# MLP down projection: all 16 pairs of row blocks by seven products, and a last product that is finished tile by tile

## Chip, core and metric

One core of one Trainium2 chip runs the whole layer in one launch. The metric is the device time of that launch in microseconds (us), lower is better. The time before is the median of three runs; the profile is one further execution with the hardware profiler.

The engines are named as in the profile: PE (TensorE, with PEld for its weight loads), DVE (VectorE), ACT (ScalarE), POOL (GpSimd) and SP (SyncE, which here only issues DMA transfers). SBUF is the on-chip memory of 128 partitions, PSUM the eight banks of 128x512 float32 into which PE sums.

## What is computed

The layer is a streaming encoder step over 1024 prompt rows and 128 sample rows, 1152 tokens of width 1024. The change touches only its last part, which in the reference is one line of `finish`:

```python
u = jnp.square(jax.nn.relu(jnp.einsum('bld,df->blf', rmsnorm(h, g_pre_mlp), w_up)))
return h + rmsnorm(jnp.einsum('blf,fd->bld', u, w_down), g_post_mlp)
```

`w_up` is 1024 x 4096 and `w_down` 4096 x 1024, so `u` is 1152 x 4096. Float32 accuracy is reached with float32r operands: each operand is split into a high part (an ACT copy to float32r) and a low part (the difference, one DVE or POOL subtraction), and each product is three matmuls, high by high, high by low, low by high.

## The kernel before

The 4096 inner columns are 32 blocks of 128. **Up.** The first four blocks (`NCL = 4`) are made classically: `mlp_up_pe` computes them in three chunks of 384 tokens each, `up_square_act` squares them into the two buffers `ust`, and `up_store` writes each to the scratch `c_scr`. The other 28 blocks are 14 pairs (`NPAIR = 14`), each made from seven block products in the manner of Strassen and Winograd: `pair_pe` runs products 1, 6, 7, 5, then the last 128 tokens (`last_tokens_pe`), 4, a turn of those tokens (`last_turn_pe`), 2 and 3. `pair_dve` makes the sums of weights for the next pair, the low parts (`w_low_dve`), and the sums of results (`c22_dve` and others); `last_square_dve` squares the last tokens before the turn. After each pair `out_sums_dve` makes four sums of the squared blocks, and SP stores the pair's buffer to `u_scr`.

While the classical blocks 2 and 3 run on PE, DVE makes the weight and token sums of the first pair (`x_difference_dve`, `x_second_dve`, `x_fourth_dve`, `w_s1_dve` and so on), one instruction after another in the order of the `vector` block.

**Down.** The 14 pairs are contracted with `w_down` by seven products in the order `ZORD = (1, 7, 6, 5, 4, 2, 3)`. Product p runs over all 14 pairs (`z_step_pe`, 98 steps, `ZN = 7 * NPAIR`) into four PSUM banks for tokens 0 to 511, three matmuls each; four of the seven also have one tile for the last 128 tokens. A step is thus 12 or 15 matmuls of 128x512. Four sets of operands (`zop[n % 4]`) go round: SP loads (`z_load_sp`), ACT makes the high parts (`z_hi_act`), DVE the low ones (`z_low_dve`), and `z_out_dve` adds each finished product into the output tiles `yt` during the next product.

**Tail.** The four classical blocks are then contracted classically: `tail_pe` runs 9 token tiles by 2 halves by 4 blocks by 3 matmuls, 216 in all, half a tile at a time. So every half tile has 12 matmuls of its own, and while PE does the next ones, the tile before is finished: `tail_dve` adds the half into `yt`, ACT squares the tile with a row sum, DVE makes the variance and its reciprocal (`norm_var`, L2681 to L2683), ACT the root, DVE one Newton step (`norm_newton`, L2687 to L2689), POOL multiplies by `g_post_mlp` (`end_gain_pool`; DVE does it for the last two tiles), and DVE multiplies by the root and adds the residual `hend` (`end_dve`). SP then stores the tile.

What sets the order: every engine runs its own queue strictly in the order in which the code is written, and waits there on semaphores. There is no scheduler.

Of the kernel before, what the change touches and what calls it, by code (L numbers as in the profile page):

```python
# [5 lines left out]
P = 128  # L6
# [6 lines left out]
D = 1024  # L13
# [27 lines left out]
NTAIL = NCL // 2  # L41
# [158 lines left out]
def layer(nc, I, O, scratch):  # L200
    o_scr, sig_scr, h_scr = scratch
    keep = ExitStack()
    with keep:
# [173 lines left out]
        wr[0] = wr_first + [raw[x][:, 512 * h:512 * h + 512] for x in range(2) for h in range(2)] + wr_late  # L377

        class Operands:
            def __init__(self, k):  # L380
# [7 lines left out]
        sb("before_yt", [P, 1152], ctx=D1)  # L388
# [4 lines left out]
        uraw = [osT_rl[:, 0:TOK], sb("uraw1", [P, TOK], ctx=D1)]  # L393
# [4 lines left out]
        tu = [[sb(f"tu{b}{x}", [P, 2 * TOK], F32R, E1) for x in range(2)] for b in range(2)]  # L398
        td1h = sb("td1h", [P, 2 * D], F32R, E1)
        sb("before_td1l", [P, 3840], ctx=E1)  # L400
        td1l = sb("td1l", [P, 2 * D], F32R, E1)
        sb("before_hend8", [P, 2048], ctx=E1)
        hend8 = sb("hend8", [P, D], ctx=E1)
        jend = sb("jend", [P, D], ctx=E1)
        sb("before_hend", [P, 6400], ctx=E1)
        hend = [sb(f"hend{t}", [P, D], ctx=E1) for t in range(8)] + [hend8]
        gend = sb("gend", [P, D], ctx=E1)
        E1.close()
        yg = raw
        td = [[[wh[0][:, :], wh[1][:, :]], [wl[0][:, :], wl[1][:, :]]],  # L410
              [[T[:, D * x:D * x + D] for x in range(2)] for T in (td1h, td1l)]]
        cum_scr = nc.dram_tensor("cum_scr", (STREAMS * HEADS, PK), F32, kind="Internal").ap()
        c_scr = nc.dram_tensor("c_scr", (NCL * P, TOK), F32, kind="Internal").ap()
        u_scr = nc.dram_tensor("u_scr", (NPAIR * P, UCOL), F32, kind="Internal").ap()
# [61 lines left out]
        u_lo, u_hi, u_down, d_hi, d_lo = sem("u_lo"), sem("u_hi"), sem("u_down"), sem("d_hi"), sem("d_lo")  # L476
        u_out, u_in, d_in, rw_in = ([sem(f"{n}{x}") for x in range(2)] for n in ("u_out", "u_in", "d_in", "rw_in"))
# [5 lines left out]
        yg_done, yg_last = sem("yg_done"), sem("yg_last")  # L483
# [2339 lines left out]
        def up_store(sp, j):  # L2823
            sp.wait_ge(u_lo, U_B + (j + 5 if j < 2 else 3 * j + 3))
            sp.dma_start(c_scr[P * j:P * j + P, :], ust[j % 2]).then_inc(u_out[j % 2], 16)
# [281 lines left out]
        def ust_free(eng, Q, x):  # L3107
            eng.wait_ge(u_out[x], Q.of((32, 16)[x], U0))
# [150 lines left out]
        def pair_sp(sp, Q):  # L3259
            if Q.it is None:  # L3260
                rows = slice(P * Q.n0, P * Q.n0 + P)
            else:
                rows = bass.ds(Q.of(P), P)
# [26 lines left out]
        ZN = 7 * NPAIR  # L3290
# [12 lines left out]
        def zprod(n):  # L3303
            return ZORD[n // NPAIR]
# [19 lines left out]
        def z_load_sp(sp, n):  # L3324
            i, s, k = zprod(n), n % NPAIR, n % 4
# [3 lines left out]
            if n < 4:  # L3329
                sp.wait_ge(q_done, 9 * (NPAIR - 1) + (2, 3, 3, 4)[n])  # L3330
                sp.wait_ge(u_out[0], U0 + 32 * (s + 1))
# [4 lines left out]
            if n == NPAIR - 1:  # L3336
                sp.wait_ge(u_out[0], U1)
                sp.wait_ge(u_out[1], U2)
            rows = slice(P * s, P * s + P)
            for x, b, h in ZLOAD.get(i, ()):  # L3340
                f = P * (NCL + 2 * s + b)
# [5 lines left out]
        def z_sum_dve(v, n):  # L3347
            i, s = zprod(n), n % NPAIR
            to, a, b, op = ZSUM[i]
            v.wait_ge(z_in[n % 4], z_in_at(n))  # L3350
            v.wait_ge(q_low, Z_LOW + z_parts_at(n - NPAIR))
            nc.vector.tensor_tensor(wr[to][s][:, :], wr[a][s][:, :], wr[b][s][:, :], op).then_inc(q_sum, 1)

        def z_hi_act(act, n):
            i, s, Z = zprod(n), n % NPAIR, zop[n % 4]
            act.wait_ge(z_in[n % 4], z_in_at(n))
            if n < 4:
                act.wait_ge(q_done, 9 * (NPAIR - 1) + (2, 3, 3, 4)[n])
            else:
# [4 lines left out]
            nc.scalar.activation(Z.u[0][:, :], Z.uraw[:, :], ACT.Copy).then_inc(q_hi2, 1)  # L3364
            if i in ZLAST:
                nc.scalar.activation(Z.last[0][:, :], Z.lraw[:, :], ACT.Copy).then_inc(q_hi2, 1)

        def z_low_dve(v, n):
            i, s, Z = zprod(n), n % NPAIR, zop[n % 4]
# [4 lines left out]
            nc.vector.tensor_tensor(Z.u[1][:, :], Z.uraw[:, :], Z.u[0][:, :].bitcast(F32), ALU.subtract).then_inc(q_low, 1)  # L3374
            if i in ZLAST:
                v.wait_ge(q_hi2, Z_HI + at_ + 3)
                nc.vector.tensor_tensor(Z.last[1][:, :], Z.lraw[:, :], Z.last[0][:, :].bitcast(F32), ALU.subtract).then_inc(q_low, 1)

        def z_step_pe(pe, n):
            p, s, Z = n // NPAIR, n % NPAIR, zop[n % 4]  # L3380
            i, own, other = zprod(n), ZBANK[p % 2], ZBANK[1 - p % 2]
            start, stop = s == 0, s == NPAIR - 1
# [32 lines left out]

        L_, R_ = slice(0, 512), slice(512, 1024)
# [14 lines left out]
        def z_out_dve(v, p, xs_):  # L3431
# [3 lines left out]
            if xs_[0] == 0:  # L3435
# [626 lines left out]
```

## Time and profile before

| | us |
|---|---|
| time, median of 3 runs (1632.14 to 1632.45) | 1632.45 |
| the profiled execution's own time | 1632.51 |
| its span, first to last instruction | 1630.6 |
| mean granted PE clock over the span | 0.998 |

The engines' busy shares of the span are PE 99%, DVE 65%, ACT 48%, POOL 20%. A start time in a row is counted from the start of the span. A duration of a PE, DVE or ACT instruction can reach into the next one's; from one start to the next is what an instruction costs in a row of them.

### The profile page before, as it was taken

How to read it: one execution, taken by the hardware profiler on the slowest of the kernel's cores; microseconds unless marked ns; L12 is line 12 of the kernel's file. 1: busy time of each engine (PE TensorE's matmuls, PEld its weight loads, DVE VectorE, ACT ScalarE, POOL GpSimd, SP SyncE). 2: the span in 40 equal slices, each digit the busy share in tenths (PEclk: the TensorE clock that was granted, in tenths of full speed). 3: DMA queues.
4: the chain of work that ended last, by engine and by line, in shares of the span. 5: the costliest groups of instructions: out<-in, count | busy, mean ns of one | idle time of the engine just before them, and what ended most of it. 6: DMA issues, size and time to landing. Idle time of an engine off the chain costs nothing.

```text
span 1630.6 us, 27195 instructions
## 1 busy us (share of the span) xinstructions
PE 1614.9 (99%) x9314; PEld 1465.3 (90%) x9314; DVE 1064.4 (65%) x2323; ACT 782.7 (48%) x1643; POOL 329.5 (20%) x539
## 2 busy tenths in 40 slices
PE   8999999999999999999999999999999999999998
PEld 8999999999999999999988998888888888888886
DVE  7567777645888422264455798887787577775657
ACT  6487887865888523341343452222222334344522
POOL 0412312225544322234522100000000000000124
PEclk9999999999999999999999999999999999999999
DMA  5221312322222556654433424433444773353642
GB/s 185 82 63 38 84 48 65 90 91 55 69 73 74 195 193 203 208 194 153 140 122 95 141 82 149 148 122 119 144 134 155 242 241 102 109 171 105 187 157 117
DMA packets 167437, 209.73 MB, mean 129 GB/s; under 512 B 16697, under 2 KB 114361, under 8 KB 167329
## 3 DMA queue, kind: packets, MB, share of 16 engines
q1 hardware_dynamic: 167328, 208.34, 40.1%
q8 instruction: 61, 1.00, 0.3%
q14 instruction: 48, 0.39, 0.1%
HBM read 148.26 MB, written 58.24 MB: 127 GB/s over the span
## 4 chain that ended last, share of the span: by engine, by line
PE 95%; DVE 2%; ACT 2%; issue 0%; DMA 0%; SPq 0%; DVEq 0%; ACTq 0%
PE gb L565 9%; PE gb L3395 6%; PE sc L3395 6%; PE gb L2488 6%; PE gb L1024 5%; PE gb L1026 5%; PE gb L1025 5%; PE gb L3044 5%; PE sc L3044 5%; PE tp L3395 5%; PE tp L3044 5%; PE tp L864 4%; PE sc L2647 3%; PE gb L2870 3%; PE tp L2647 3%; PE gb L3054 2%
## 5 line engine op out<-in xcount | busy, mean ns | idle before, releaser
L534 POOL TENSOR_TENSOR wl<-raw,wh 128x256 fp32r<-128x256 f32 x168 | 123.3, 759 | 299.9 <-ACT wh L516 175.7
L1024 PE MATMUL gb<-Xh,wh 128*128 128x384 f32 (+1 forms) x504 | 173.0, 343 | 0.0
L1025 PE MATMUL gb<-Xh,wl 128*128 128x384 f32 (+1 forms) x504 | 170.8, 339 | 0.0
L1026 PE MATMUL gb<-Xl,wh 128*128 128x384 f32 (+1 forms) x504 | 170.8, 339 | 0.0
L3516 POOL TENSOR_TENSOR wl<-raw,wh 128x1024 fp32r<-128x1024 f32 x2 | 5.3, 2626 | 624.8 <-ACT wh L3507 624.8
L565 PE MATMUL gb<-Xh,wh 128*128 128x384 f32 (+1 forms) x288 | 102.8, 357 | 0.0
L565 PE MATMUL gb<-Xh,wl 128*128 128x384 f32 (+1 forms) x288 | 97.6, 339 | 0.0
L3395 PE MATMUL gb<-zw,zu 128*128 128x512 f32 x378 | 97.2, 389 | 0.0
L565 PE MATMUL gb<-Xl,wh 128*128 128x384 f32 (+1 forms) x288 | 97.2, 338 | 0.0
L1024 PEld LDWEIGHTS gb<-Xh,wh 128*128 128x128 f32 x504 | 94.8, 188 | 0.4
L1025 PEld LDWEIGHTS gb<-Xh,wl 128*128 128x128 f32 x504 | 94.8, 188 | 0.1
L1026 PEld LDWEIGHTS gb<-Xl,wh 128*128 128x128 f32 x504 | 94.8, 188 | 0.0
L3395 PE MATMUL sc<-zw,zu 128*128 128x512 f32 x336 | 89.5, 389 | 0.0
L3395 PE MATMUL tp<-zw,zu 128*128 128x512 f32 x336 | 85.3, 389 | 0.0
L3395 PEld LDWEIGHTS gb<-zw,zu 128*128 128x128 f32 x378 | 70.9, 188 | 14.7
L3363 ACT ACTIVATE zw<-wr 128x512 fp32r<-128x512 f32 x56 | 35.4, 632 | 91.5 <-issue 45.8
L3395 PEld LDWEIGHTS sc<-zw,zu 128*128 128x128 f32 x336 | 63.1, 188 | 13.1
L3395 PEld LDWEIGHTS tp<-zw,zu 128*128 128x128 f32 x336 | 63.1, 188 | 13.1
L3374 DVE TENSOR_TENSOR zu<-zr,zu 128x512 fp32r<-128x512 f32 x98 | 67.1, 684 | 0.0
L3372 DVE TENSOR_TENSOR zw<-wr,zw 128x512 fp32r<-128x512 f32 x56 | 46.0, 822 | 27.0 <-ACT zw L3363 26.7
L2488 PE MATMUL gb<-Oh,wh 128*128 128x384 f32 x188 | 63.2, 336 | 0.2 <-DVE Ol L2437 0.2
L2488 PE MATMUL gb<-Ol,wh 128*128 128x384 f32 x188 | 62.8, 334 | 0.0
(551 smaller groups left out, 4637.6 us busy)
## 6 DMA issues: line engine op xcount, KB each, us to landing
zr<-u_scr SPq DMA_DIRECT2D x98, 256.0 KB, 3.0
raw<-in_w_in SPq DMA_DIRECT2D x70, 256.0 KB, 3.3
u_scr<-ustore SPq DMA_DIRECT2D x28, 576.0 KB, 3.9
u_scr<-ustore SPq DMA_DIRECT2D x14, 768.0 KB, 3.3
sig_scr<-sig SPq DMA_DIRECT2D x16, 576.0 KB, 3.2
raw<-in_w_up SPq DMA_DIRECT2D x36, 256.0 KB, 4.6
kc<-in_cache_fox_k SPq DMA_DIRECT2D x8, 1024.0 KB, 5.5
vc<-in_cache_fox_v SPq DMA_DIRECT2D x8, 1024.0 KB, 7.7
```

The lines of the kernel that those rows point to most:

```text
L534: last = nc.gpsimd.tensor_tensor(wl[U.slot][:, q], raw[U.slot][:, q], wh[U.slot][:, q].bitcast(F32), ALU.subtract)
L565: last = nc.tensor.matmul(bank[:, 0:b - a], w_[U.slot][:, ws], x_[:, k, a:b], start=(k == 0 and j == 0), stop=(k == KT - 1 and j == 2))
L864: last = nc.tensor.transpose(four(rbank[R.slot])[0:n, j, 0:m], src, ident[0:m, 0:m])
L1024: nc.tensor.matmul(bank[:, 0:x1 - x0], wh[U.slot][:, ws], Xh3[:, k, x0:x1], start=(k == 0), stop=False)
L1025: nc.tensor.matmul(bank[:, 0:x1 - x0], wl[U.slot][:, ws], Xh3[:, k, x0:x1], start=False, stop=False)
L1026: last = nc.tensor.matmul(bank[:, 0:x1 - x0], wh[U.slot][:, ws], Xl3[:, k, x0:x1], start=False, stop=(k == KT - 1))
L2488: last = nc.tensor.matmul(bank[:, 0:384], w_[M.U.slot][:, ws], x_[:, 4 * y + k, a:b], start=(k == 0 and j == 0), stop=(k == 3 and j == 2))
L2647: last = nc.tensor.matmul(bank[:, :], m_[:, k, ts], w_[:, hs], start=(k == 0 and j == 0), stop=(k == KT - 1 and j == 2))
L2870: last = nc.tensor.matmul(gb[x][:, 0:384], w_[j % 2][:, ws], x_[:, k, a:a + 384], start=(k == 0 and i == 0), stop=(k == KT - 1 and i == 2))
L3044: last = nc.tensor.matmul(bank[:, :], w_of(i, wp)[:, P * k:P * k + P], x_of(i, xp)[:, k, :], start=(k == 0 and j == 0), stop=(k == 3 and j ...
L3374: nc.vector.tensor_tensor(Z.u[1][:, :], Z.uraw[:, :], Z.u[0][:, :].bitcast(F32), ALU.subtract).then_inc(q_low, 1)
L3395: last = nc.tensor.matmul(bank[:, :], A[a], Z.w[w][:, :], start=(start and j == 0), stop=(stop and j == 2))
```

## The change

All 32 blocks go through the seven products (`ZP = NPAIR + NCL // 2 = 16` pairs, `ZN = 112` steps), and the classical tail is gone with its loads and splits.

1. The first four blocks are still made classically, but as two more pairs: POOL makes the four sums that `out_sums_dve` makes for the others (`up_sums_pool`), and SP stores them into `u_scr`. The squares of blocks 2 and 3 wait for sums and store of blocks 0 and 1, since they share `ust`. ACT squares the first two chunks of block 2 a little later than before, behind a split for the pair.
2. Loads of `w_down` for pairs 14 and 15 have buffers of their own; the last two steps have operands of their own (`EndOperands`).
3. The last step of the last product (`z_group_pe`, `GROUP = 1`) raises a semaphore for each tile, in the order 8, 1, 2, 3, 0.
4. Tiles 4 to 7 (`EARLY`) are complete before the last product; their squares, variances, gains and residuals are put between the steps of the last product. `g_post_mlp` and `hend` are loaded during the last two products. The left halves of the five late tiles are squared and multiplied there too.
5. The five late tiles are finished in `end_late_dve`, one after the other, behind the last product. POOL makes all gains, DVE none.

```diff
+ZP = NPAIR + NCL // 2
+GROUP = 1
...
+        def up_sums_pool(pool, b):
+
+            add = nc.gpsimd.tensor_tensor
+            t1_, t2_ = slice(0, HALF), slice(HALF, SEQ)
+            pool.wait_ge(u_lo, U_B + 6 * b + 6)
+            if b:
+                pool.wait_ge(u_out[0], 16)
+            add(usum[0], ust[0][:, t2_], ust[1][:, t2_], ALU.add).then_inc(uc_sum, 1)
+            pool.wait_ge(uc_sum, 4 * b + 1)
+            add(ust[0][:, t2_], ust[0][:, t1_], ust[0][:, t2_], ALU.subtract).then_inc(uc_sum, 1)
+            pool.wait_ge(uc_sum, 4 * b + 2)
+            add(usum[1], usum[0], ust[0][:, t1_], ALU.subtract).then_inc(uc_sum, 1)
+            pool.wait_ge(uc_sum, 4 * b + 3)
+            add(usum[2], ust[1][:, t1_], usum[1], ALU.subtract).then_inc(uc_sum, 1)
...
-            if j >= 2:
-                act.wait_ge(u_out[j % 2], 16 * (j // 2))
+            if j == 2:
+                act.wait_ge(uc_sum, 3)
+                act.wait_ge(uc_out, 16)
+            elif j == 3:
+                act.wait_ge(u_out[1], 16)
...
-        ZN = 7 * NPAIR
+        ZN = 7 * ZP
...
+        def z_group_pe(pe):
+
+
+            for t in (8,) + ZTILES:
+                for n in range(ZN - GROUP, ZN):
+                    Z = zset(n)
+                    if t == 8:
+                        pe.wait_ge(q_low, Z_LOW + z_parts_at(n))
+                        bank, A = ZBANK[1][1], [l_[:, :] for l_ in Z.last]
+                    else:
+                        bank, A = ZBANK[0][t], [u_[:, P * t:P * t + P] for u_ in Z.u]
+                    for j, (a, w) in enumerate(((0, 0), (0, 1), (1, 0))):
+                        last = nc.tensor.matmul(bank[:, :], A[a], Z.w[w][:, :], start=False, stop=(n == ZN - 1 and j == 2))
+                last.then_inc(z_tile, 1)
...
-        def tail_pe(pe):
-            for b in range(NTAIL):
-                pe.wait_ge(u_down, 2 * b + 2)
-                pe.wait_ge(d_lo, 2 * b + 2)
-                for q in range(6):
-                    if b == 0 and q == 3:
-                        pe.wait_ge(q_step, Z_OUT + z_out_at(7))
-                    last = tail_product_pe(b, ENDB[q], q // 2, q % 2)
-                    if b == NTAIL - 1:
-                        last.then_inc(dn_full, 1)
-            for q in range(6, 2 * TT):
-                pe.wait_ge(dn_free, END_B + q - 5)
-                for b in range(NTAIL):
-                    last = tail_product_pe(b, ENDB[q % 6], q // 2, q % 2)
-                last.then_inc(dn_full, 1)
...
+        END_FROM = 6 * ZP + 4
+        EARLY, LATE = (4, 5, 6, 7), (8,) + ZTILES
+        FINAL = EARLY + LATE
...
+            end_square_act(act, LATE[0], 1)
+            for x in range(1, 5):
+                end_square_act(act, LATE[x], 1)
+                end_root_act(act, LATE[x - 1])
+            end_root_act(act, LATE[4])
...
+            for t in EARLY:
+                pool.wait_ge(sq_b, sq_at(t, 1))
+                nc.gpsimd.tensor_tensor(yt[t][:, :], yt[t][:, :], gend[:, :], ALU.mult).then_inc(yg_done, 1)
+            for h in range(2):
+                for t in LATE:
+                    pool.wait_ge(sq_b, sq_at(t, h))
+                    nc.gpsimd.tensor_tensor(half(yt[t], h), half(yt[t], h), half(gend, h), ALU.mult).then_inc(yg_done, 1)
...
+        def end_late_dve(v):
+
+
+            z_out_last_dve(v, 6)
+            for x in range(5):
+                end_var_dve(v, LATE[x])
+                if x < 4:
+                    z_out_dve(v, 6, (x,))
+                end_newton_dve(v, LATE[x])
+                end_dve(v, LATE[x])
...
@@ -3903,8 +3904,7 @@
             pairs(v, lambda Q: pair_dve(v, Q), NPAIR)
             z_steps_dve(v)
-            z_out_dve(v, 6, range(4))
-            end_group_dve(v, lambda t, h: tail_dve(v, t, h))
+            end_late_dve(v)
...
@@ -3953,9 +3953,8 @@
-            for b in range(NTAIL):
-                for x in range(2):
-                    tail_low_pool(pool, b, x)
+            for b in range(2):
+                up_sums_pool(pool, b)
             end_gain_pool(pool)
```

How the instructions stand, at the places where the order matters. On POOL, from the last residual sum of the stage before (L2754, in the change L2749) to the end of the queue; `tb` and `xr` are the residual's buffers. Before:

```order
L2754 TENSOR_TENSOR tb0<-tb0,xr0 128x1024
L3516 TENSOR_TENSOR wl0<-raw0,wh0 128x1024
L3516 TENSOR_TENSOR wl1<-raw1,wh1 128x1024
L3516 TENSOR_TENSOR td1l<-raw0,td1h 128x1024
L3516 TENSOR_TENSOR td1l<-raw1,td1h 128x1024
L3599 TENSOR_TENSOR raw0<-yt0,gend 128x1024
```

And in the change:

```order
L2749 TENSOR_TENSOR tb0<-tb0,xr0 128x1024
L2825 TENSOR_TENSOR ustore<-ustore 128x512
L2827 TENSOR_TENSOR ustore<-ustore 128x512
L2829 TENSOR_TENSOR ustore<-ustore 128x512
L2831 TENSOR_TENSOR ustore<-ustore 128x512
L2825 TENSOR_TENSOR ustore<-ustore 128x512
L2827 TENSOR_TENSOR ustore<-ustore 128x512
L2829 TENSOR_TENSOR ustore<-ustore 128x512
L2831 TENSOR_TENSOR ustore<-ustore 128x512
L3622 TENSOR_TENSOR yt4<-yt4,gend 128x1024
```

The four splits of the tail's weights are gone; eight half-width sums of the first blocks stand in front of the gains.

On DVE, the end of the queue: `yt` is an output tile, `hend` its residual, `small` the columns of the norm. Before, tiles 7 and 8:

```order
L3606 TENSOR_TENSOR raw1<-yt7,gend 128x1024
L2681 TENSOR_SCALAR small<-small 128x1
L2682 TENSOR_SCALAR small<-small 128x1
L2683 RECIPROCAL small<-small 128x1
L3551 TENSOR_TENSOR yt8<-tp0,yt8 128x512
L2687 TENSOR_SCALAR small<-small 128x1
L2688 TENSOR_SCALAR small<-small 128x1
L2689 TENSOR_SCALAR small<-small 128x1
L3627 SCALAR_TENSOR_TENSOR yt7<-raw1,small,hend7 128x1024
L3551 TENSOR_TENSOR yt8<-tp1,yt8 128x512
L3606 TENSOR_TENSOR raw0<-yt8,gend 128x1024
```

In the change, the turn of tile 1, the second of five late ones:

```order
L3644 SCALAR_TENSOR_TENSOR yt8<-yt8,small,hend8 128x1024
L2676 TENSOR_SCALAR small<-small 128x1
L2677 TENSOR_SCALAR small<-small 128x1
L2678 RECIPROCAL small<-small 128x1
L3517 TENSOR_TENSOR yt2<-tp0,yt2 128x512
L2682 TENSOR_SCALAR small<-small 128x1
L2683 TENSOR_SCALAR small<-small 128x1
L2684 TENSOR_SCALAR small<-small 128x1
L3644 SCALAR_TENSOR_TENSOR yt1<-yt1,small,hend1 128x1024
```

Each late tile's turn holds the addition of the next tile's last product between its reciprocal and its Newton step, and ends in the residual of the whole tile.

On ACT, the end of the queue in the change (L3588 squares half a tile, L3592 is the root):

```order
L3588 ACTIVATE gb0,small<-yt8 128x512
L3588 ACTIVATE gb0,small<-yt1 128x512
L3592 ACTIVATE small<-small 128x1
L3588 ACTIVATE gb0,small<-yt2 128x512
L3592 ACTIVATE small<-small 128x1
L3588 ACTIVATE gb0,small<-yt3 128x512
L3592 ACTIVATE small<-small 128x1
L3588 ACTIVATE gb0,small<-yt0 128x512
```

Tile 8's root stands behind tile 1's square, tile 1's behind tile 2's, and so on. Before, each root followed its own tile's square.

## Rows read from the trace of the kernel before

**Rows 1.** The page, busy time of the engines (share of the span, instructions).

```profile
PE 1614.9 (99%) x9314; PEld 1465.3 (90%) x9314; DVE 1064.4 (65%) x2323; ACT 782.7 (48%) x1643; POOL 329.5 (20%) x539
```

**Rows 2.** Chain that ended last, in order of time, its end: start, length, what.

```profile
1573.67 2.72 PE gb L3522 x12
...
1614.47 2.73 PE sc L3522 x12
...
1617.30 0.06 DVE yt L3551
```

**Rows 3.** Timeline, DVE, to the end: start, length, instruction, [idle before <-releaser].

```profile
1543.84 2.55 DVE L3372 TENSOR_TENSOR zw<-wr,zw 128x512 fp32r<-128x512 f32 x1 [0.27 <-ACT zw L3363]
...
1562.05 0.29 DVE L3377 TENSOR_TENSOR zl<-zs,zl 128x128 fp32r<-128x128 f32 x1
...
1620.24 0.21 DVE L2681 TENSOR_SCALAR small<-small 128x1 f32<-128x1 f32 x1
...
1620.75 0.67 DVE L3551 TENSOR_TENSOR yt<-tp,yt 128x512 f32<-128x512 f32 x1
...
1622.07 1.28 DVE L3627 SCALAR_TENSOR_TENSOR yt<-raw,small,hend 128x1024 f32<-128x1024 f32 x1
1623.27 0.69 DVE L3551 TENSOR_TENSOR yt<-tp,yt 128x512 f32<-128x512 f32 x1
...
1625.14 0.21 DVE L2681 TENSOR_SCALAR small<-small 128x1 f32<-128x1 f32 x1
...
1626.00 0.27 DVE L2687 TENSOR_SCALAR small<-small 128x1 f32<-128x1 f32 x1 [0.27 <-ACT small L3589]
...
1626.75 1.42 DVE L3631 SCALAR_TENSOR_TENSOR yt<-raw,small,hend 128x512 f32<-128x512 f32 x2
```

**Rows 4.** Timeline, ACT, the last tile's second half.

```profile
1623.99 0.63 ACT L3586 ACTIVATE jend<-yt 128x512 f32<-128x512 f32 x1 [1.76 <-DVE yt L3551]
1624.53 0.19 ACT L3586 ACTIVATION_READ_ACCUMULATOR jend<-yt 128x1 f32 x1
1625.77 0.20 ACT L3589 ACTIVATE small<-small 128x1 f32<-128x1 f32 x1 [1.05 <-DVE small L2683]
```

**Rows 5.** Timeline, POOL, last stage: two passes over 128x1024.

```profile
1543.21 2.62 POOL L3516 TENSOR_TENSOR wl<-raw,wh 128x1024 fp32r<-128x1024 f32 x1 [4.17 <-ACT wh L3507]
...
1585.45 2.40 POOL L3599 TENSOR_TENSOR raw<-yt,gend 128x1024 f32<-128x1024 f32 x1 [26.02 <-DVE yt L3551]
```

**Rows 6.** Timeline, all engines, mixing stage: DVE and POOL together.

```profile
740.25 1.84 DVE L2505 SCALAR_TENSOR_TENSOR Ml<-sga,Mh 128x384 f32 x2
...
740.41 1.26 POOL L2514 TENSOR_TENSOR sga<-sga,sgb 128x384 f32<-128x384 f32 x1 [1.06 <-DVE sgb L2498]
```

**Rows 7.** Stretches: PE, PEld, DVE, ACT, POOL busy (instructions), PEclk granted, DMA share.

```profile
935.00:958.00 23.00, 23.00 (x135) 23.00 (x134) 22.69 (x24) 12.17 (x20) 0.00 (x0) 1.00 0.30 98
1624.00:1626.00 2.00, 0.00 (x0) 0.00 (x0) 1.66 (x4) 0.92 (x3) 0.00 (x0) 0.73 0.64 262
```

**Rows 8.** Timeline, ACT, squares that end first-block pairs 0 and 1.

```profile
934.71 0.51 ACT L2886 ACTIVATE ustore<-osT_rl 128x384 f32<-128x384 f32 x1
...
958.85 0.53 ACT L2886 ACTIVATE ustore<-osT_rl 128x384 f32<-128x384 f32 x1
```

**Rows 9.** Timeline, DVE, from the last first-block work into the first pair.

```profile
955.38 1.29 DVE L3036 TENSOR_TENSOR wq<-rw,wq 128x512 fp32r<-128x512 f32 x2
...
964.28 0.69 DVE L3000 TENSOR_TENSOR ss<-raw 128x512 f32<-128x512 f32 x1
...
969.34 0.68 DVE L3183 TENSOR_TENSOR ustore<-tp,vsum 128x512 f32<-128x512 f32 x1
...
972.54 0.43 DVE L3161 TENSOR_TENSOR rs<-rs 128x256 f32<-128x256 f32 x1 [0.59 <-ACT rs L3123]
```

**Rows 10.** Timeline, PE, start of the first pair, and its turn of tokens.

```profile
958.13 0.63 PE L3044 MATMUL sc<-Mh,wq 128*128 128x512 f32 x2
...
974.68 0.38 PE L3060 MATMUL gb<-ident,rs 128*128 128x128 f32 x2
```

More of the change, by code:

```diff
@@ L387, in layer @@
         zop = [Operands(3)]
-        sb("before_yt", [P, 1152], ctx=D1)
+        wr[2] += [sb(f"wr_last{s}", [P, 512], ctx=D1) for s in range(2)]
+        sb("before_yt", [P, 128], ctx=D1)
         yt = [sb(f"yt{t}", [P, D], ctx=D1) for t in range(6)] + yt_last
@@ L392, in layer @@
         sb("before_uraw", [P, 384], ctx=D1)
-        uraw = [osT_rl[:, 0:TOK], sb("uraw1", [P, TOK], ctx=D1)]
+        wr[1] += [sb(f"wr_end{s}", [P, 512], ctx=D1) for s in range(2)]
         D1.close()
@@ L3107, in ust_free @@
         def ust_free(eng, Q, x):
+            if Q.first():
+                eng.wait_ge(uc_out, 32)
             eng.wait_ge(u_out[x], Q.of((32, 16)[x], U0))
@@ L3303, in zprod, with __init__, zset @@
         def zprod(n):
-            return ZORD[n // NPAIR]
+            return ZORD[n // ZP]
+        class EndOperands:
+            def __init__(self, k):
+                side = (wh, wl)[k]
+                self.w = [side[0][:, 0:512], side[0][:, 512:1024]]
+                self.u = [side[1][:, 0:512], side[1][:, 512:1024]]
+                self.last = zlast[k]
+        zend = [EndOperands(k) for k in range(2)]
+        def zset(n):
+            return zend[n - ZN + 2] if n >= ZN - 2 else zop[n % 4]
         def parts_in(n):
@@ L3514, in tail_low_pool @@
-        def tail_low_pool(pool, b, x):
-            pool.wait_ge(d_hi, 2 * b + x + 1)
-            nc.gpsimd.tensor_tensor(td[b][1][x], raw[x][:, :], td[b][0][x].bitcast(F32), ALU.subtract).then_inc(d_lo, 1)
-        def tail_product_pe(b, bank, t, h):
-            for x in range(2):
-                us = slice(TOK * x + P * t, TOK * x + P * t + P)
-                for i, (up, dp) in enumerate(((0, 0), (0, 1), (1, 0))):
-                    last = nc.tensor.matmul(bank[:, :], tu[b][up][:, us], td[b][dp][x][:, 512 * h:512 * h + 512],
-                                            start=(b == 0 and x == 0 and i == 0), stop=(b == NTAIL - 1 and x == 1 and i == 2))
-            return last
@@ new lines, in end_square_act @@
+        def end_square_act(act, t, h):
+            if sq_at(t, h) > TT + 1:
+                act.wait_ge(sq_b, sq_at(t, h) - 1)
+            if t in EARLY:
+                act.wait_ge(q_step, Z_OUT + z_out_at(6))
+            elif h == 0:
+                act.wait_ge(q_step, Z_OUT + z_out_at(6))
+            else:
+                act.wait_ge(q_step, Z_OUT + z_out_at(6) + LATE.index(t) + 1)
+            c = (32, 75)[h] + t
+            nc.scalar.activation(junk_bank[:, :], half(yt[t], h), ACT.Square, accum_out=stat[:, c:c + 1]).then_inc(sq_b, 1)
@@ L3815, in _ @@
             pairs(act, lambda Q: pair_act(act, Q), NPAIR)
[L3816 to L3821 removed]
+            z_steps_act(act)
         @block.vector
@@ L3993, in _ @@
             pairs(pe, lambda Q: pair_pe(pe, Q), NPAIR)
-            for n in range(ZN):
+            for n in range(ZN - GROUP):
                 z_step_pe(pe, n)
-            tail_pe(pe)
+            z_group_pe(pe)
 def tables():
```

263 lines of the change are left out of this document (103 added, 160 removed).

## Prediction

> **What bounds the kernel now.** I read the page first, then the chain, then the two places where the change puts new work. PE is busy for 99% of the span [rows 1], and the end of the chain is nothing but its matmuls [rows 2]: the tail starts at 1573.67, and sixteen half tiles of 12 matmuls each end at 1617.20 (1614.47 + 2.73). That is 43.53 us for 192 matmuls, 0.2267 us each. The last two half tiles end PE's work at 1617.20 + 24 x 0.2267 = 1622.64. The span is 1630.6, so 7.96 us follow the last matmul. Two things can therefore change the time: the number of matmuls (if nobody makes PE wait), and the length of what follows the last one. A third is a new wait of PE at a place where its supplier has no room. The reader is to see in [rows 7] that DVE is such a supplier: from 935 to 958 it is busy for 22.69 of 23.00 us.
>
> **Matmuls removed.** The tail's 216 go. Two more pairs through seven products cost 2 x 7 x 4 x 3 = 168, and 2 x 4 x 3 = 24 for the last tokens, 192 together. 24 fewer, at 0.2267: **-5.44 us**. The tail's splits on ACT, DVE and POOL lay beside PE and give nothing back. Loads grow from 14 to 16 per product at the same rate per step, so I cost them at nothing; the loads run four steps ahead, and if that cover were gone a step would wait for its transfer.
>
> **POOL's sums beside a full DVE.** POOL and DVE cannot both read two SBUF operands. In [rows 6] DVE starts at 740.25 two instructions of 384 columns; POOL starts 0.16 later and ends at 741.67; the DVE pair ends at 742.09, 0.42 behind POOL, after 1.84 us. One of them would need about 0.45 to 0.5 by the 0.60 that 512 columns take from one start to the next [rows 9]. So I read that POOL waited for the first, and the second for POOL. In [rows 3] and [rows 5] POOL works from 1543.21 to 1545.83, and the DVE subtraction of 1543.84 takes 2.55 us, ending 0.56 after POOL, where its like takes 0.69.
>
> The Trainium skill ("SBUF — State Buffer", who interferes with whom) says the same: the port pair is an exclusive lock for a whole instruction, and a DVE instruction with two SBUF inputs contends with a GpSimd instruction that reads SBUF. The trace agrees (2.55 against 0.69 us). The rule speaks against putting sums on POOL where DVE is full.
>
> A POOL pass over 128x1024 takes 2.40 [rows 5]; one over 512 at least half, 1.20, and 1.30 with some fixed cost (384 columns take 1.26 in [rows 6], a wait of about 0.25 among it). I take 1.30. It delays a full DVE by about 0.1 less, 1.19. The first four sums can start when the last square of block 1 ends, 934.71 + 0.51 = 935.22 [rows 8]. Each needs the one before, so they alternate with DVE instructions of 0.6 to 1.2 us and are through by about 944. DVE is then 4 x 1.19 = 4.75 behind. The low part of weight 1, which started at 955.38 [rows 9], would start at 960.1. But the second four sums start when the last square of block 3 ends, 959.4 [rows 8] and some 0.2 later here, so one of them gets in front of it: done at about 962.05. PE began product 1 at 958.13 [rows 10]. It waits about 4.0 us.
>
> The other three sums fall on DVE before it reaches the first pair's weights for the next. From 964.28 on [rows 9] it is 4.75 + 4 x 1.19, less about 1 us that it idled between, so 8.5 us late. `c22_dve` moves from 969.34 to 977.85, and three instructions and one low part later the square of the last tokens starts at 980.4 instead of 972.54 (there it had waited 0.59 for ACT) and ends at 980.8. PE's turn of tokens, 974.68 before [rows 10], stands behind it: PE arrives at 978.7 and goes on at 980.9. PE is thus **+6.2 us** late in all, the first wait being part of it. After that DVE has idle time in each pair and catches up. What is queued behind PE's waits is all of PE's later work. Bounds: 0, if the POOL sums find gaps or their delay is covered; 10, if each sum costs DVE a full alternation. The stores of the sums come at 944 and 968 and are asked for only at `c22_dve`: hidden. SP stands in these stores with the next pair's weight load behind it, which is wanted over 15 us later.
>
> A wait of 4 us can also cost clock. After PE's last matmul (1622.64) the granted clock of the stretch from 1624 to 1626 is 0.73 [rows 7], half-way between the full level (2.4 GHz) and the half (1.2 GHz): it fell some 2 us after the work ended. If it falls in the first wait, product 1 may take twice its 12 x 0.2267 = 2.72 us. PE would then arrive at 981.4 instead of 978.7, only 0.5 later than DVE lets it go. I take 0 and keep 0 to 3.
>
> **The last product.** Four early tiles add to DVE, each in two steps (30 matmuls, 6.8 us), variance 0.51, Newton step 0.75, residual 1.20 (all [rows 3], start to start), and at most 2.4 of POOL's lock: 4.9. With the low parts of two steps, about 3.0 by the 0.6 of [rows 9], that is 7.9 against 6.8, so 4.4 us late after four. DVE finished its last low part at 1562.34 [rows 3], and PE began the last step at 1573.67 - 15 x 0.2267 = 1570.27: 7.9 us ahead. The cover holds, cost nothing; if it were gone, up to 4.4.
>
> **After the last matmul.** Let E be PE's end. Tile 8 is ready at E - 2.72. Its addition starts 0.10 later as in [rows 2]; the square starts 0.72 after the addition and is done 0.73 after that [rows 3, 4]. Then the variance (0.51) and the addition of tile 1, at E - 0.59. ACT's root for tile 8 stands behind tile 1's square, which is done at E + 0.86; Newton starts 0.23 later [rows 3, 4] and the residual could start at E + 1.84. But POOL has begun tile 1's gain (1.30) at E + 0.95 and holds the lock till about E + 2.2. The residual takes 1.20: tile 8 ends at E + 3.4. Tiles 1, 2, 3 each take: variance 0.51, next addition 0.72, square 0.73, root 0.23, Newton 0.75, that is 2.94; POOL's gain ends at 3.3; residual 1.20: 4.5 us, three times, E + 16.9. Tile 0: 0.86 from variance to Newton, 0.75, and 3.85 from the residual to the end of the span (1626.75 to 1630.6) [rows 3]: 5.46. The end is E + 22.4, against E + 7.96 before: **+14.4 us**. Without POOL's lock the turns are 3.04 and 4.14, and it is +13.0. With nothing but DVE's own work in the turns (3.07 each) it is +8.3; if each turn waits for one more full lock, about +17.
>
> **Sum.** -5.44 + 6.2 + 14.4 = +15.2: span 1645.8. The execution's own time lies 1.9 above its span, 1647.7, and the median 0.06 below that execution: **1647.6**.
>
> **Rivals.**
> - *POOL's sums are covered* and only the end is longer: -5.44 + 14.4 gives 1641.5. For it: in z steps a blocked DVE cost PE nothing (2.55 at 1543.84 with PE busy throughout). Against: there DVE was far ahead, here it has about 2 us to PE (low part 1 ready 956.1, wanted 958.1).
> - *More pile-up*: the sums cost more than one pass each, or the clock falls and stays low for more than one product: front +10 to +13, 1651 to 1656. For it: two separate waits.
> - *ACT and POOL round trips hide* and turns are DVE's work alone, front hidden as well: -5.44 + 8.3, 1635.3, no difference that counts. Against: the order on ACT puts each root behind the next square.
> - *Faster*: the late tiles are finished under the last matmuls, and what follows E is one tile's chain as now, 7.96 us. Then only the matmuls count: 1627.0. With the front hidden it decides at a turn of about 1.5 us (3.4 + 3 x 1.5 + 5.5 = 13.4 = 7.96 + 5.44); the turns have at least 3.07 of DVE work, and PE gives a tile each 0.68. I see no way there.
> - *It does not do what it says*: the queue shows the 24 fewer matmuls and no tail; nothing speaks for this.
>
> **Chances.** Forecast (front 3 to 9, end 12.5 to 16) 0.70; sums covered 0.17; more pile-up 0.06; DVE-only turns 0.03; faster 0.03; something unseen 0.01. The range takes in the covered case from its lower side, 1639.0, and reaches to 1653. A measurement of this kernel can tell 0.2%, 3.3 us, from no change. Faster by more 0.03, within 0.04, slower 0.93.
>
> **What would show it.** Right: POOL rows of about 1.3 us between 935 and 968, DVE instructions of 1.8 to 1.9 us beside them; PE's first pair starting near 962 and its turn near 981; PE's end near 1630.6 - 7.96 - 5.44 + 6.2 = 1623.4; DVE residuals 4.5 us apart after it; 22 us from the last matmul to the end. Wrong: no PE wait there (covered), a shorter end with roots right behind their own squares, or PE waits in the last two products for operands or for transfers.

## The result and the profile after

The changed kernel takes 1645.3 us (median of 6 runs, 1645.1 to 1648.2), the kernel before on the same chip 1632.3 (6 runs). The ratio is 1.0083, with a 95% interval of 1.0070 to 1.0096: slower by 13 us, as the forecast had it in sign, and 2.3 us under the forecast time of 1647.6. The profiled execution took 1645.37 with a span of 1643.6, 13.0 longer than the 1630.6 before.

The busy time of the engines on the page, which answers to [rows 1]:

```profile
PE 1611.8 (98%) x9290; PEld 1462.1 (89%) x9290; DVE 1082.5 (66%) x2350; ACT 792.2 (48%) x1685; POOL 336.9 (20%) x550
```

24 matmuls are gone, as the diff says. What came in their place is seen at two spots. The first is the front of the pairs. POOL's timeline, the first six of the eight sums (columns: start, length, instruction, idle time before it and who ended it):

```profile
935.02 1.42 POOL L2825 TENSOR_TENSOR ustore<-ustore 128x512 f32<-128x512 f32 x1 [19.49 <-ACT ustore L2903]
936.52 2.15 POOL L2827 TENSOR_TENSOR ustore<-ustore 128x512 f32<-128x512 f32 x1
938.75 2.16 POOL L2829 TENSOR_TENSOR ustore<-ustore 128x512 f32<-128x512 f32 x1
940.99 2.15 POOL L2831 TENSOR_TENSOR ustore<-ustore 128x512 f32<-128x512 f32 x1
959.18 1.28 POOL L2825 TENSOR_TENSOR ustore<-ustore 128x512 f32<-128x512 f32 x1 [16.05 <-ACT ustore L2903]
960.54 1.61 POOL L2827 TENSOR_TENSOR ustore<-ustore 128x512 f32<-128x512 f32 x1
```

DVE's timeline in the same stretches:

```profile
934.06 1.23 DVE L2969 TENSOR_TENSOR xs<-xs,Ml 128x1024 f32<-128x1024 f32 x1
935.21 2.32 DVE L2857 TENSOR_TENSOR wl<-raw,wh 128x1024 fp32r<-128x1024 f32 x1
937.45 2.31 DVE L2967 TENSOR_TENSOR xs<-Mh 128x1024 f32<-128x1024 f32 x1
939.79 2.20 DVE L2968 TENSOR_TENSOR xs<-xs,Ml 128x1024 f32<-128x1024 f32 x1
942.02 2.19 DVE L2969 TENSOR_TENSOR xs<-xs,Ml 128x1024 f32<-128x1024 f32 x1
944.14 1.21 DVE L2992 TENSOR_TENSOR t<-xs,t 128x1024 fp32r<-128x1024 f32 x1
...
959.25 3.45 DVE L3053 TENSOR_TENSOR wq<-rw,wq 128x512 fp32r<-128x512 f32 x2
...
976.21 0.69 DVE L3202 TENSOR_TENSOR ustore<-tp,vsum 128x512 f32<-128x512 f32 x1
```

The reader sees four DVE instructions of 2.2 to 2.3 us between neighbours of 1.2: from the first of them (935.21) to the next free one (944.14) it is 8.93 us, where the same four take 4.79 with POOL out of the way (experiment below): 1.04 more for each POOL sum. The fifth and sixth sums fall on the low parts of the first weights, the first of which PE waits for: 3.45 for two, which took 1.29 in [rows 9]. The last row is the first instruction of `c22_dve`, at 969.34 before. PE's timeline, and behind it stretches of one microsecond (first number after the comma: PE busy; the number after POOL's is the granted clock):

```profile
961.06 1.22 PE L3061 MATMUL sc<-Mh,wq 128*128 128x512 f32 x2 [3.04 <-DVE wq L3053]
...
979.21 0.44 PE L3077 MATMUL gb<-ident,rs 128*128 128x128 f32 x2
```

```profile
960.00:961.00 1.00, 0.00 (x0) 0.00 (x0) 1.00 (x2) 1.00 (x2) 0.92 (x2) 0.78 0.00 0
961.00:962.00 1.00, 0.94 (x2) 0.84 (x3) 1.00 (x2) 0.09 (x1) 1.00 (x1) 0.50 0.00 0
962.00:963.00 1.00, 1.00 (x4) 0.73 (x3) 1.00 (x2) 0.00 (x0) 0.92 (x2) 0.50 0.00 0
963.00:964.00 1.00, 1.00 (x4) 0.81 (x3) 1.00 (x1) 0.00 (x0) 0.92 (x2) 0.51 1.03 429
964.00:965.00 1.00, 1.00 (x5) 0.82 (x5) 0.97 (x2) 0.00 (x0) 1.00 (x1) 1.00 0.48 178
```

PE stands still for about 3.2 us (3.04 by the row), the granted clock falls from its full level (2.4 GHz) to the half (1.2), and product 1 ends at 965.27, 4.21 after its start. Behind a wait of 3.03 with the clock at 1.00 it took 2.86 (962.22 to 965.08 in the root-first run below), so the clock cost it 1.35. Everything up to here starts 0.28 earlier than in the trace before. Such shifts ahead of the changed code reach 1.9 us between the traces of this document, so the figures below are counted from an anchor in the same trace. Counted from ACT's last square of block 1 (934.43; 934.71 before, [rows 8]) the turn of tokens comes after 44.78 us, against 39.97 before ([rows 10]): the front costs **4.8**.

The second spot is the end. The chain that ended last (start, length, what):

```profile
1619.80 1.37 PE tp L3464 x6
1621.21 0.70 DVE yt L3517
1622.00 0.72 ACT gb L3588 x2
1622.84 0.28 DVE small L2682
...
1623.59 1.55 DVE yt L3644
...
1627.92 1.55 DVE yt L3644
...
1636.59 1.55 DVE yt L3644
...
1639.66 0.75 DVE yt L3649
```

The six matmuls of 1619.80 end at 1621.17, and three more, 0.68, end PE's work at 1621.85. From there on the path is DVE, ACT, DVE in turns of 4.33 us. In ACT's and POOL's timelines the second turn reads:

```profile
1626.33 0.60 ACT L3588 ACTIVATE gb<-yt 128x512 f32<-128x512 f32 x1 [3.52 <-DVE yt L3517]
...
1626.96 0.19 ACT L3592 ACTIVATE small<-small 128x1 f32<-128x1 f32 x1
1627.13 1.26 POOL L3626 TENSOR_TENSOR yt<-yt,gend 128x512 f32<-128x512 f32 x1 [3.07 <-ACT gb L3588]
```

The root (L3592) comes behind the next tile's square (L3588), and POOL's gain runs from 1627.13 to 1628.39, into the residual of 1627.92. In all, 21.75 us follow PE's end, against 7.96 before: **+13.8**. The sum is -5.44 + 4.8 + 13.8 - 0.28 = +12.9, of the 13.0 measured.

### The profile page after: what moved, and what is told of

It reads as the page before. It is cut to its first block, busy times and chain, and to the rows that moved or that the text cites. A ratio compares the mean times of both kernels' runs of the same rounds, so it can differ in the third digit from the quotient of the medians.

```text
span 1643.6 us, 27261 instructions
## 1 busy us (share of the span) xinstructions
PE 1611.8 (98%) x9290; PEld 1462.1 (89%) x9290; DVE 1082.5 (66%) x2350; ACT 792.2 (48%) x1685; POOL 336.9 (20%) x550
## 4 chain that ended last, share of the span: by engine, by line
PE 92%; DVE 5%; ACT 2%; DMA 1%; issue 0%; SPq 0%; DVEq 0%; ACTq 0%
PE gb L560 9%; PE gb L3431 7%; PE sc L3431 7%; PE gb L2483 5%; PE tp L3431 5%; PE gb L1019 5%; PE gb L1021 5%; PE gb L1020 5%; PE sc L3061 5%; PE gb L3061 5%; PE tp L3061 5%; PE tp L859 4%; PE sc L2642 3%; PE tp L2642 3%; PE gb L3071 2%; PE po L3061 2%
## 5 line engine op out<-in xcount | busy, mean ns | idle before, releaser
L3622 POOL TENSOR_TENSOR yt<-yt,gend 128x1024 f32<-128x1024 f32 x4 | 11.6, 2892 | 619.7 <-ACT gb L3588 619.7
L3431 PE MATMUL gb<-zw,zu 128*128 128x512 f32 x432 | 111.0, 389 | 0.0
L3431 PE MATMUL sc<-zw,zu 128*128 128x512 f32 x372 | 98.9, 389 | 0.0
L3431 PEld LDWEIGHTS gb<-zw,zu 128*128 128x128 f32 x432 | 81.1, 188 | 16.8
L3431 PE MATMUL tp<-zw,zu 128*128 128x512 f32 x372 | 94.4, 389 | 0.0
L3431 PEld LDWEIGHTS sc<-zw,zu 128*128 128x128 f32 x372 | 69.8, 188 | 14.5
L3431 PEld LDWEIGHTS tp<-zw,zu 128*128 128x128 f32 x372 | 69.8, 188 | 14.5
L3410 DVE TENSOR_TENSOR zu<-zr,zu 128x512 fp32r<-128x512 f32 x110 | 77.6, 705 | 0.0
L3400 ACT ACTIVATE zu<-zr 128x512 fp32r<-128x512 f32 x110 | 67.8, 616 | 0.0
```

Source lines behind the costliest of these rows:

```text
L3400: nc.scalar.activation(Z.u[0][:, :], zop[n % 4].uraw[:, :], ACT.Copy).then_inc(q_hi2, 1)
L3410: nc.vector.tensor_tensor(Z.u[1][:, :], zop[n % 4].uraw[:, :], Z.u[0][:, :].bitcast(F32), ALU.subtract).then_inc(q_low, 1)
L3431: last = nc.tensor.matmul(bank[:, :], A[a], Z.w[w][:, :], start=(start and j == 0), stop=(stop and j == 2))
```

## The experiments

All start from the changed kernel (1645.3). "Turn" below is the turn of the last tokens, counted from the anchor, ACT's last square of block 1; "E" is the end of PE's last matmul.

### POOL writes and doesn't read

```diff
-            add = nc.gpsimd.tensor_tensor
+            def add(out, a_, b_, op):
+                return nc.gpsimd.memset(out, 0.0)
```

> Left out: the eight sums of block 1 to 4 of the first pair of the down product. POOL's eight instructions stay, in number, place and size, but each only writes zeros and reads nothing, so the outputs are not the reference's. My theory is that a POOL sum costs because it reads two SBUF operands while DVE does the same (DVE's 1.22 us become 2.2 to 2.3). Then, with no reads on POOL, DVE's instructions beside it keep 1.2 us, the first weight's low part is 4.1 us earlier, PE's idle time of 3.2 us before the first pair goes below 0.5, the granted clock stays at 1.00, and the last tokens' turn falls back by about 4.5: median 1640.8 (1640 to 1642). Rival: DVE is late because it has more to wait for (ACT's squares, the stores of the sums, the order of queues), not by the reads: then PE still waits about 3 us and the time stays at 1645.3.

1640.28 (4 runs). POOL's first four writes, and DVE's timeline beside them:

```profile
934.85 2.29 POOL L2821 MEMSET ustore<- 128x512 f32 x4 [19.48 <-ACT ustore L2904]
...
935.06 1.22 DVE L2858 TENSOR_TENSOR wl<-raw,wh 128x1024 fp32r<-128x1024 f32 x1
936.19 1.22 DVE L2968 TENSOR_TENSOR xs<-Mh 128x1024 f32<-128x1024 f32 x1
```

None is longer than usual (starts at 935.06 and, four on, 939.85: the 4.79 above), PE doesn't wait, the turn is back at 39.97, exactly the figure of the kernel before. So the whole 4.8 goes with POOL's reads. The stores of the sums and ACT's squares, which wait for the same semaphores here, cost nothing by themselves. One thing more changes in this run: a write takes 0.57 us and a sum about 1.3, so the stores and squares are also released earlier. The next run, whose instructions on POOL are longer, narrows that down.

### POOL copies one operand

```diff
+                return nc.gpsimd.tensor_copy(out, a_)
```

> Left out: the eight sums. POOL's eight instructions each copy their first operand (one SBUF operand read) instead of adding two, so the outputs are not the reference's. It tells whether POOL must read two operands to hold DVE up or whether one does. If any read takes the lock that a DVE instruction with two SBUF operands wants, DVE's 1.22 us become 1.8 to 2.3 beside the copies, PE again waits 1.5 to 3 us before the first pair: 1642.5 to 1645. If only two reads do it, it is as with eight writes: no DVE instruction over 1.3, no wait, 1640.3.

1640.61 (one run). Neither end of the expectation: DVE's instructions take 1.52 to 1.63, and that still fits into the slack; PE doesn't wait (turn 39.97). POOL's first four copies and DVE's timeline:

```profile
934.90 5.41 POOL L2821 COPY ustore<-ustore 128x512 f32<-128x512 f32 x4 [19.48 <-ACT ustore L2904]
...
935.10 1.63 DVE L2858 TENSOR_TENSOR wl<-raw,wh 128x1024 fp32r<-128x1024 f32 x1
936.66 1.63 DVE L2968 TENSOR_TENSOR xs<-Mh 128x1024 f32<-128x1024 f32 x1
```

So one operand that POOL reads is enough to hold DVE up, 0.36 us per copy (four take 6.21, not 4.79) against 1.04 per sum. The Trainium skill ("SBUF — State Buffer", who interferes with whom) says that a DVE instruction with two SBUF inputs contends with a GpSimd instruction that reads SBUF, and not with one that only writes it. The traces agree: 1.22 beside writes, 1.52 to 1.63 beside copies, 2.2 to 2.3 beside sums. That DVE loses less to a copy than to a sum goes with the copy's length. The first of the four, which starts ahead of DVE's instruction, takes 0.75 us where a sum takes 1.28; the other three take 1.49 each, POOL's own wait for DVE included. So a second operand read by POOL need not cost anything beyond the time that it adds; no run here separates the two. Four copies keep POOL for 5.4 us (the sums 8.1), and neither they nor the stores behind them make PE wait: a busy POOL queue by itself is not the cause of the 4.8.

### DVE makes the sums

```diff
             up_low_dve(v, 3)
+            up_sums_dve(v, 0)
...
             x_fourth_dve(v, 1)
+            up_sums_dve(v, 1)
...
-            for b in range(2):
-                up_sums_pool(pool, b)
```

> The eight sums of the first pair are made by DVE itself, four behind weight 3's low part and four in the second half of the activations' work; POOL has none. If a POOL sum costs DVE about 1.07 us each by waiting, then DVE's own sums, 0.6 to 0.65 each, are cheaper although DVE now does all the work: c22 about 3 us earlier than 976.2, PE's first wait near 1 us and no fall of the clock, the turn of tokens near 976: median 1642.3 (1641 to 1643.5). Rival: POOL's sums run beside DVE for the most part (the usual reason to use POOL), and giving them to DVE adds 8 x 0.62 = 5 us to an engine that was full: 1647 or more.

1642.40 (4 runs), as my theory had it: four sums of its own take DVE 2.78 us (936.10 to 938.88), 0.70 each (I had 0.60 to 0.65), less than the 1.04 that it loses to each of POOL's. PE's waits in this stretch (total, times, longest):

```profile
PE gb L3077 <- DVE rs L3180: 1.0, 1, 1.0
PE sc L3061 <- DVE wq L3053: 0.6, 1, 0.6
```

The granted clock stays at 1.00 behind the wait of 0.6. The turn comes after 41.96 us, 2.0 behind the kernel before: DVE is still too full there.

### The clock kept up

```diff
             B = Q.next(-1)
+            if Q.first():
+                pe.wait_ge(dn_free, DB)
+                for _ in range(12):
+                    nc.tensor.matmul(bank7[:, :], Mh3[:, 4, 0:P], Mh3[:, 4, 0:HALF], start=True, stop=True)
             w_ready(pe, Q, 1)
```

> Twelve matmuls of 128x512 whose results nobody reads are put on PE ahead of its wait for the first pair's weights, into a bank that is free there, so that PE doesn't idle for 3.2 us before product 1 and the granted clock does not fall. In the changed kernel product 1 takes 4.21 us instead of 2.73, with the granted clock at 0.50 from 961 to 964. My theory: those 1.48 us cost next to nothing, because the turn of the last tokens (979.21) waits for DVE's square (978.74 + 0.42) anyway; PE would only arrive there 1.5 earlier and wait that much longer: product 1 takes 2.73, clock 1.00, the turn stays within 0.3 of 979.2, median 1645.1 (1644.9 to 1645.5). Rival: the clock is on the path; then the turn comes at 977.8 and the median is 1643.8.

1645.23 (5 runs): no change. The clock reads 1.00 through product 1, PE arrives earlier at the turn and waits there, as its timeline shows:

```profile
978.98 0.44 PE L3077 MATMUL gb<-ident,rs 128*128 128x128 f32 x2 [1.35 <-DVE rs L3184]
```

Turn after 44.81, as in the changed kernel. The 1.35 us that the clock had cost product 1 (I had 1.48, against a product without a wait before it) lay beside DVE's own lateness. The root-first run below says the same without any edit here: in its trace the same wait of 3.03 us left the clock at 1.00, PE waited 1.35 at the turn, and the turn came after 44.77.

### Root before the next square

```diff
             for x in range(1, 5):
-                end_square_act(act, LATE[x], 1)
                 end_root_act(act, LATE[x - 1])
+                end_square_act(act, LATE[x], 1)
```

> One edit on ACT's order after the last matmul: the root of a tile comes before the square of the next tile, not behind it. My theory: the turn of 4.33 us between residuals is a chain of DVE, ACT, DVE because the root stands behind the next square. With the root first the next square runs beside the Newton step, and the turn is DVE's own work: variance 0.51, addition 0.7, Newton 0.75, residual 1.2, 3.1 to 3.3 us. First residual 0.8 earlier and three turns 1.1 shorter: -4.1, median 1641.2 (1640.5 to 1642.5). Rival: POOL's gain of 1.26 us with its two SBUF operands falls on every residual; then DVE waits for it wherever the root stands, turns stay at 4.2 or more, and the time is 1644.5 to 1645.3.

1641.17 (4 runs). DVE's timeline, the residuals of the first two late tiles:

```profile
1623.68 1.28 DVE L3644 SCALAR_TENSOR_TENSOR yt<-yt,small,hend 128x1024 f32<-128x1024 f32 x1
...
1626.72 1.28 DVE L3644 SCALAR_TENSOR_TENSOR yt<-yt,small,hend 128x1024 f32<-128x1024 f32 x1
```

ACT's, the root now ahead of the next square:

```profile
1625.51 0.20 ACT L3592 ACTIVATE small<-small 128x1 f32<-128x1 f32 x1 [1.66 <-DVE small L2678]
1626.15 0.60 ACT L3588 ACTIVATE gb<-yt 128x512 f32<-128x512 f32 x1 [0.44 <-DVE yt L3517]
```

And POOL's, the gain beside the first residual:

```profile
1623.92 2.16 POOL L3626 TENSOR_TENSOR yt<-yt,gend 128x512 f32<-128x512 f32 x1 [0.77 <-ACT gb L3588]
```

The turn is 3.04, DVE's own work. In its trace 16.7 us follow PE's end instead of 21.75: the first residual 0.85 earlier, three turns 1.29 shorter, 0.3 at the last. The contention hasn't gone: it changed sides. POOL's gain now begins 0.24 after the residual and takes 2.16 instead of 1.26, where nobody waits for it. That is why the residual fell from 1.55 to 1.28. Of the 1.29 that a turn loses, 0.27 is this, and 1.02 is DVE's wait for ACT, which is gone. The time fell by 4.1 and not by 5.0: in its profiled execution PE's work ends 0.9 later, and the anchor, ahead of the changed code, already lies 1.2 later.

### Three and six steps tile by tile

```diff
-GROUP = 1
+GROUP = 3
```

> One number: the last three steps of the last product, and not only the last one, are made tile by tile. PE then ends a tile every 2.04 us, not every 0.68, and the tile of the last tokens is ready 5.4 us earlier. If what follows is a sequence of turns of 4.33 us that starts with that tile, the whole sequence starts 5.44 us earlier against PE's end and nothing else moves: 16.3 us from the last matmul to the end, not 21.75: median 1639.9 (1639 to 1641). The last low part is made by 1611.0, and PE would want it at about 1613, so PE doesn't wait. Rival: DVE's cover of low parts is thinner than I read, PE waits for one of them and 2 to 3 us of the gain are lost (1642 to 1643); or the end is set by the last tile's own work and nothing changes (1645.3).

1640.43 (4 runs), 4.9 less, and 16.6 us after E (1623.54 to 1640.1 in its trace, whose anchor lies 1.7 later than the changed kernel's). PE doesn't wait for a low part. The turns themselves are as before (residuals at 1620.08, 1624.44, 1628.78, 1633.11); the row of them only starts 5.2 earlier against PE. With `GROUP = 6`:

> As the run with the last three steps tile by tile, but with the last six, nothing else changed. PE gives a tile every 4.08 us, about a turn (4.33), so nearly all of the turns lie beside matmuls: 9.4 us from the last matmul to the end, 12.3 less. But the tile of the last tokens then wants the low part of the last step about 1601.4 + 5 x 0.68 = 1604.8, and DVE, which is busy without a gap from 1578 to 1611, has it at 1611.0: PE waits about 6 us. So, on the changed kernel's 1645.3, -12.3 + 6.2 = 1639.2 (1638 to 1640.5). Rival: DVE's order leaves room to make the last low parts earlier, PE waits under 1 us: 1633 to 1634.

1641.99 (4 runs), 2.8 above my figure. PE waits at the first tile of the group, as expected, but that is not all it costs. Its timeline, and then its stretches of five microseconds (PE busy, granted clock, DMA share and GB/s):

```profile
1605.64 0.96 PE L3464 MATMUL gb<-zw,zl 128*128 128x512 f32 x3 [2.84 <-DVE zl L3413]
1608.24 1.65 PE L3464 MATMUL gb<-zw,zl 128*128 128x512 f32 x3 [1.64 <-DVE zl L3413]
...
1612.50 3.36 PE L3464 MATMUL sc<-zw,zu 128*128 128x512 f32 x12
```

```profile
1600.00:1605.00 5.00, 2.80 (x13) 1.00 0.59 210
1605.00:1610.00 5.00, 2.73 (x7) 0.66 0.67 275
1610.00:1615.00 5.00, 5.00 (x15) 0.65 0.00 0
```

PE is idle for 4.47 us of the first ten (I had 6.2), and its clock is 0.66 and 0.65 of full in the two stretches from 1605 to 1615. Its end is at 1629.29, and without wait it would have been 1621.55 (this trace runs 0.3 ahead): 7.74 late, of which 3.3 are not idle time. Some 2.7 of them lie where the clock is down: the nine matmuls from 1608.24 to 1612.50 take 4.26 us where nine at 0.2267 take 2.04, and the twelve behind them 3.19 where 2.72 is usual. Here the clock is on the path, since PE waits for nobody behind it. The rest of the miss is after E: 10.5 us, not 9.4.

### Three edits together, and where POOL's late gains stand

DVE's sums, root first and `GROUP = 4` in one kernel.

> Three edits together, computing all of the reference: DVE makes the eight sums; ACT takes each root before the next square; the last four steps go tile by tile. From the single runs: the front gives 3.0, as with DVE's sums alone. At the end PE gives a tile every 2.72 us, the turn is 3.04, so the first residual comes at E - 7.4, the fourth at E + 1.7, and the end at E + 8.4 instead of E + 21.75: -13.3. Against that, PE wants the last low part about 0.75 before DVE has it. Sum on 1645.3: 1629.8 (1629 to 1631), 0.15% faster than the kernel before (1632.4). Rival: the edits take from each other (the low parts are late by more, since the late gains of POOL run beside them, or turns stretch while PE works): 1632 to 1634, no gain over the kernel before.

1631.08 (11 runs), ratio to the kernel before 0.9991 (0.9982 to 1.0000). 9.3 us after E, turns of 3.04, and one wait of 0.44 in PE's waits:

```profile
PE gb L3464 <- DVE zlast L3413: 0.4, 1, 0.4
```

That is 1.3 us above the sum of the single gains. About 0.4 of it is before E: PE loses 1.1 around that low part, where I had 0.75. And 0.9 is after it, for a reason that I had overlooked: the first residual stands behind the addition of the second tile in DVE's queue, and that addition waits for PE, as DVE's timeline shows:

```profile
1612.14 0.69 DVE L3517 TENSOR_TENSOR yt<-sc,yt 128x512 f32<-128x512 f32 x1 [0.67 <-PE sc L3464]
```

Then one wait more on POOL, with four and with five steps:

```diff
+            pool.wait_ge(q_low, Z_LOW + z_parts_at(ZN - 1))
             for h in range(2):
                 for t in LATE:
```

> As the run before, with four steps tile by tile as in the combination, so that against the combination only the time of POOL's five gains differs. Theory: the wait of 0.44 and the loss of 0.9 go, the rest stays: 9.0 us after the last matmul, median 1630.0 (1629.5 to 1630.8). Rival: gains moved behind the low parts delay the first late tile: 1631 or more.

1630.00 (11 runs), ratio 0.9985 (0.9976 to 0.9994): the lowest median of all, 0.15% below the kernel before. That is clear of noise, but less than the 0.2% from which the prediction counts a change. Its interval overlaps that of the run before, so only the trace tells the two apart: PE waits for no low part, and from the anchor to E it takes 1.1 us less; 9.3 us follow E in both. Of the 5.44 that the matmuls give, this kernel keeps about 2.1: 2.0 go at the front and 1.3 behind E.

> The combination of three edits (DVE's sums, root first, last steps tile by tile) with five such steps instead of four, and with one wait more: POOL starts the left halves' gains of the five late tiles only when DVE has made the last low part. In the combination these five stood from about 1597 to 1605 beside the low parts, which then took 1.04 to 1.78 instead of 0.68 and 1.38 instead of 0.28, about 5 us of DVE in all, and PE waited 0.44 and lost 0.9 in all for a low part. My theory: with the gains out of the way the last low part is made near 1604, PE doesn't wait even with five steps, the matmuls end at about 1619.1, a tile comes every 3.40, longer than the turn of 3.04, and 8.1 to 8.5 us follow the last matmul: span 1627.5, median 1629.3 (1628.8 to 1630.3), 0.18% faster than the kernel before. Rival: the gains now fall on the first late tiles' additions and residuals instead, so what DVE gains before it loses behind (1631 or more); or the low parts are held by PE's own progress, not by DVE's load, and PE waits at tile 8 as before.

1630.75 (11 runs), ratio 0.9990 (0.9981 to 0.9999), 0.45 above the range that I gave. PE's side came out as expected (last low part at 1603.7, no wait, E at 1618.70), but the rival was right about what follows: 9.8 us after E, since the gains that were moved now stand in the way of the first late tile's residual. DVE's timeline:

```profile
1611.71 2.20 DVE L3645 SCALAR_TENSOR_TENSOR yt<-yt,small,hend 128x1024 f32<-128x1024 f32 x1 [1.63 <-POOL yt L3627]
```

## Why the prediction was right, step by step

- **Matmuls, -5.44**: held. With POOL's reads gone, the span is 1638.5; that is 1630.6 - 5.44 + 13.8 - 0.4 (its earlier start), within 0.1.
- **Front, +6.2, measured +4.8**: mechanism and place right, size too large. The term that was mis-sized is what a sum costs a full DVE: 1.19, measured 1.04. The length of a sum was right: taken as 1.30, and 1.28 for the fifth one, which hardly waits. Too small was the overlap of the two engines, taken as 0.1: in the alternation, POOL ends 1.12 after DVE's instruction (939.79 to 940.91), and DVE's next one starts 1.11 after that (942.02), where DVE alone takes 1.20. The error goes through eight sums: DVE is 4.1 late after four, not 4.75; the first wait is 3.2 instead of 4.0; `c22_dve` is 7.15 late instead of 8.5; the turn 4.8 instead of 6.2.
- **A sign of its own that did not hold**: the prediction wanted DVE instructions of 1.8 to 1.9 us beside POOL's. The rows show 2.2 to 2.3. The figure fits the narrow instructions (0.68 and 1.19); for those of 128x1024, which stand there, its own 1.19 on top of 1.2 would have given 2.4.
- **Clock, 0 to 3, taken as 0**: it fell and cost product 1 1.35 us, yet nothing in the total. The reason given (PE would arrive 0.5 after DVE let it go) would have made it 0.5, so the 0 was partly luck: with the clock kept up, PE waits exactly 1.35 at the turn. Two runs (clock kept up, root first) show the price to be zero here. In the runs with three and six steps the clock fell later, product 1 took 4.45 and 4.46, and the turn came after 44.88 and 44.91, about 0.1 later than 44.78. The run with six steps also shows that the price isn't zero where no supplier is late behind it.
- **Last product, early tiles at 0**: held. DVE's last low part is done at 1611.0, and PE starts the last step at 1618.44: 7.4 ahead, where my count left 3.5 (7.9 less 4.4). The outcome was right and the count was not: it left out POOL's five left-half gains of the late tiles, which stand beside the last low parts. Moved behind them (the late-gains run with four steps against the three edits together), the last low part is made 4.05 earlier, counted from the anchor. Why the early tiles cost so much less than 4.4 is not shown. The run with six steps spends this cover and pays.
- **After the last matmul, +14.4, measured +13.8**: turns 4.33 instead of 4.5, the first residual at E + 1.74. It ended at E + 3.2 (1625.06), where I had E + 3.4: it waits for POOL's gain as predicted, and is listed with 1.55 for it, not 1.28. The excess has the same source as at the front: behind POOL's gain, the residual takes 1.00 more (1628.39 to 1629.39) and not 1.20. The cause, the root behind the next square, is shown by its reversal: 3.04.
- **Rivals**: covered sums (1641.5) is what the run with POOL's writes looks like, 1640.3. DVE-only turns exist, but need ACT's other order: 3.04 measured, 3.07 forecast. That turns could be hidden under matmuls, which I saw no way to, is for the most part a matter of one number, `GROUP`. The time given for more pile-up has a slip: a front of +13 makes 1654.5, not 1656.

Left open: why the same wait of about 3 us brought the clock down within it in the changed kernel, only behind it in the traces with three and six steps, and not at all in the root-first one.

## What to carry to other kernels

Before giving work to POOL to relieve DVE, look at DVE's rows next to POOL rows that read SBUF: if each grows by more than the work would take on DVE (1.04 against 0.70 here), DVE does it cheaper itself. What follows the last matmul is a row of turns: count the turn, and see that PE delivers a tile no faster than that, at the cost of wanting the last operands earlier. In a turn over two engines, the order on the one that is mostly idle (root before or behind the next square) can set the length: 3.04 or 4.33 us here.

## What the runs showed of the hardware that I had not expected

- The granted clock is not the same for the same wait. PE idle for 3.0 us before product 1: 0.50 from 961 to 964 in the changed kernel; 1.00 all through in the root-first trace; in the trace with three steps it was still 0.97 from 962 to 963, with PE at work again, and 0.50 for the next three microseconds. Its stretches (PE busy, granted clock, DMA share and GB/s):

```profile
962.00:963.00 1.00, 0.29 (x1) 0.97 0.00 0
963.00:964.00 1.00, 1.00 (x4) 0.50 0.00 0
```

- What DVE's instructions with two SBUF operands lose to a POOL instruction depends on what that one reads: 0 beside a write of 128x512, 0.36 us beside a copy (0.75 long where it doesn't wait), 1.04 beside a sum (1.28 long); and who starts second pays (2.16 for POOL's gain, 1.28 for the residual, or 1.26 and 1.55).
